# A hybrid decoder step on one core: GpSimd multiplies three key pages of four by the query instead of two

## The chip, the cores and the metric

The kernel runs on one NeuronCore of a Trainium2 chip. The metric is the device time of one launch in microseconds. The engines are TensorE (PE, its weight loads PEld), VectorE (DVE), ScalarE (ACT), GpSimd (POOL) and SyncE (SP, which here issues nearly all DMAs); they run their own instruction streams and meet at semaphores.

## The reference

One layer for 1024 prompt tokens and 8 sample tokens that each have a paged past of 512 keys and values (4 pages of 128). The part that matters here is the samples' attention:

```python
def attend_sample(q, k, v, lam, k_past, v_past):
    s_past = jnp.einsum('bqhcd,bkhcd->bhcqk', q, k_past).astype(F32) * scale
    s_new = jnp.einsum('bqhcd,bkhcd->bhcqk', q, k).astype(F32) * scale
    p = diff_probs(jnp.concatenate([s_past, s_new], axis=-1), lam).astype(v.dtype)
    return (jnp.einsum('bhqk,bkhv->bqhv', p[..., :p_len], v_past)
            + jnp.einsum('bhqk,bkhv->bqhv', p[..., p_len:], v))

# token_mixer: both branches, merged by gates
merged = jax.nn.sigmoid(ga) * ya + jax.nn.sigmoid(gb) * yb
```

There are 8 heads with 2 groups of 64 channels each, so a past key of a sample is a row of 1024 numbers and gives 16 scores.

## The kernel before

The program has four stages, one behind the other: the norm stage, the heads stage (attention and recurrence of the prompt), the **gate stage** (`gates_stage`, L1428) and the tail stage (output projections and the MLP). The gate stage computes the last 12 tiles of the gates ga and gb with TensorE. Tile m is three pieces of 344 columns, so there are 36 pieces; one piece is 8 x 3 matmuls (`product`, L170), since every number is split into a high and a low part (products high x high, high x low, low x high). For each weight tile ScalarE makes the high part (`split`, L1590) and GpSimd the low one (`low`, L1744).

Between the pieces, one of the 8 samples' attention and recurrence steps is worked off every four pieces. `TURN_AT` sets where: at piece 4, 8, 12, ... 28, and 31 for the last. In what follows "turn i" is TensorE's place for sample i. For sample i:

- SyncE loads four key pages (`kp[0]` to `kp[3]`, 128 tokens x 1024), the query row spread over all partitions (`qB`), the sample's recurrent state (`st`), its value row (`vB`) and four value pages (`vp`).
- `keys(i)`: each page is multiplied by `qB` in place, and VectorE sums the product by 64 columns to 16 scores a token (L1783, into `s_tok`). VectorE multiplies pages 0 and 1 (L1779), GpSimd pages 2 and 3 (L1750); VectorE goes through the pages in order and waits for `k_scaled` before it reduces one of GpSimd's.
- TensorE transposes the four score blocks (`turn_scores`, L1673) as soon as the fourth reduction is done (`k_summed`), ahead of piece `TURN_AT[i]`. At sample 5 it also waits for `take_picked(0)`, a copy that VectorE makes right after `keys(5)`.
- VectorE copies the scores (L1823), takes the maximum, ScalarE the exponential (L1620), VectorE normalises, updates the recurrent state with three operations over 128 x 1024 (L1840, L1846, L1848), copies the turned probabilities (L1851), for which TensorE waits with the value products, cuts gate tiles (L1769) and starts `keys(i + 1)`. Behind sample 4 it also selects the values of four samples (L1788, L1790).
- TensorE turns the probabilities one piece after the turn (L1680), and two pieces after it makes the value products (L1691) and the state products (L1699).

All queues are written out by hand. SyncE's order for sample i: key page j of sample i + 1 once reduction j of sample i is done, the query row of i + 1 ahead of page 2, once GpSimd has made its multiplies of sample i (`k_scaled`); weights; then, each behind its wait, the value row, the state (which waits until the state of sample i is stored and used, L1512), and the value pages of i + 1. GpSimd's order: `keys(i + 1)` stands at the piece after turn i, between the low parts of the weights.

Of the kernel before, what the change touches and what calls it, by code (L numbers as in the profile page):

```python
# [44 lines left out]
PAGES = PAST // P  # L45
# [1382 lines left out]
def gates_stage(nc, a, o, c, d, xh, xl, gate, slots, x1):  # L1428
# [3 lines left out]
    with Stage(c) as ctx:  # L1432
# [26 lines left out]
        def S(n, per=1, **k):  # L1459
            return Sig(ctx, nc, f"g_{n}", per=per, **k)  # L1460
# [4 lines left out]
        k_in = [S(f"k_in{i}", step=16) for i in range(PAGES)]  # L1465
        q_in, vb_in, v_in = S("q_in", step=16), S("v_rows_in", step=16), S("v_in", PAGES, step=16)
        st_in, st_out = S("st_in", step=16), S("st_out", step=16)
        k_scaled, k_summed = S("k_scaled", 2), S("k_summed", PAGES)
        new_ready, new_done, new_read = S("new_ready"), S("new_done"), S("new_read")
        s_turned, s_max, s_exp, s_norm = S("s_turned"), S("s_max"), S("s_exp"), S("s_norm")  # L1470
        p_turned, p_read, pv = S("p_turned"), S("p_read"), S("pv")
# [32 lines left out]
        def _(sp):  # L1504
# [3 lines left out]
            def load_keys(i, j):  # L1508
                sp.dma_start(kp[j], flat(a["cache_k"][bass.ds(page_of(i, j), 1)])).then_inc(k_in[j].sem, 16)
# [4 lines left out]
            def load_spread(i):  # L1514

                sp.dma_start(qB, d["q_rows"][bass.ds(i, 1), :].broadcast_to([P, D])).then_inc(q_in.sem, 16)

            def load_values(i):
                sp.dma_start(vB, d["v_rows"][bass.ds(i, 1), :].broadcast_to([P, D])).then_inc(vb_in.sem, 16)
# [5 lines left out]
            def load_weights(m):  # L1525

                if m >= 3:
                    sp.wait_ge(w_hi.sem, w_hi.at(m - 2, 0))
                    sp.wait_ge(w_lo.sem, w_lo.at(m - 2, 0))
                src = wt[bass.ds(m + (3 + NTL * H + GATES_BEFORE), 1)] if m < N_TILES else a["w_mix"][m - N_TILES:m - N_TILES + 1]  # L1530
                sp.dma_start(raw[buf(m)][:, :], flat(src)).then_inc(w_in[buf(m)].sem, 16)

            def load_oa(k):

                sp.dma_start(x1[:, k, 0:T], flat(d["oa"][k:k + 1, :, 0:T])).then_inc(oa_in.sem, 16)
# [10 lines left out]
            for i in range(NS):  # L1546
                for j in range(PAGES):
                    sp.wait_ge(k_summed.sem, k_summed.at(i, j + 1))
                    if i + 1 < NS:
                        if j == 2:  # L1550
                            sp.wait_ge(k_scaled.sem, k_scaled.at(i, 2))
                            load_spread(i + 1)
                        load_keys(i + 1, j)
                if i + 1 == NS:
                    for k in (0, 2, 3, 4, 5):
                        load_oa(k)
                while m < N_TILES + 2 and NP * (m - 3) <= TURN_AT[i] + 1:
                    load_weights(m)
                    m += 1
                sp.wait_ge(st_new.sem, st_new.at(i, 1))  # L1560
                if i + 1 < NS:
                    load_values(i + 1)
                else:
                    load_oa(1)
                if i + 1 < NS:
                    sp.wait_ge(st_out.sem, st_out.at(i, 1))
                    sp.wait_ge(rec_out.sem, rec_out.at(i, 1))
                    load_state(i + 1)
                sp.wait_ge(pv.sem, pv.at(i, 1))
                if i + 1 < NS:  # L1570
                    load_pages(i + 1)
                else:
                    for k in (6, 7):
                        load_oa(k)
# [161 lines left out]
        @block.gpsimd  # L1736
        def _(pool):
            ctx.clear_last(pool)

            def low(m):  # L1740
                weights_in(pool, m)
                weights_free(pool, m)
                pool.wait_ge(w_hi.sem, w_hi.at(m, 0))
                pool.tensor_tensor(wlo[buf(m)][:, :], raw[buf(m)][:, :], whi[buf(m)][:, :].bitcast(F32), ALU.subtract).then_inc(w_lo.sem, 1)  # L1744

            def keys(i):
                pool.wait_ge(q_in.sem, q_in.at(i, 1))
                for j in (2, 3):
                    pool.wait_ge(k_in[j].sem, k_in[j].at(i, 1))
                    pool.tensor_tensor(kp[j], kp[j], qB, ALU.mult).then_inc(k_scaled.sem, 1)  # L1750

            low(1)
            keys(0)
            for n in range(N_PIECES):
                m, j = divmod(n, NP)
                if j == 0 and m:
                    low(m + 1)
                if n - 1 in TURN_AT and TURN_AT.index(n - 1) + 1 < NS:
                    keys(TURN_AT.index(n - 1) + 1)

        @block.vector
        def _(dve):
# [11 lines left out]
            def keys(i):  # L1774
                dve.wait_ge(q_in.sem, q_in.at(i, 1))
                for j in range(PAGES):
                    if j < 2:
                        dve.wait_ge(k_in[j].sem, k_in[j].at(i, 1))
                        ch(dve.tensor_tensor(kp[j], kp[j], qB, ALU.mult))  # L1779
                        ch.sync()  # L1780
                    else:
                        dve.wait_ge(k_scaled.sem, k_scaled.at(i, j - 1))
                    dve.tensor_reduce(s_tok[:, j, :], kp[j].rearrange("p (h n) -> p h n", n=DH), AX.X, ALU.add).then_inc(k_summed.sem, 1)  # L1783

            def select(i):
# [916 lines left out]
```

## Time and profile before

| what | value |
|---|---|
| median of 3 runs | 2424.07 us (2423.71 to 2430.54) |
| the profiled execution: time, span | 2431.48 us, 2429.7 us |
| mean granted clock of TensorE | 0.989 |
| gate stage in the span | 1185 to 1371 us |
| busy: PE, DVE, ACT, POOL | 95%, 66%, 41%, 33% of the span |
| HBM traffic | 83 GB/s over the span; 328 GB/s in the gate stage |

### The profile page before, as it was taken

To read this page: it belongs to the slowest core of one execution; us is meant where nothing else is said; L and a number is where in the kernel's file an instruction comes from. 1 tells how busy PE (TensorE), PEld (TensorE's weight loads), DVE (VectorE), ACT (ScalarE), POOL (GpSimd) and SP (SyncE) were. 2 spreads that over 40 slices of the span, in tenths; PEclk is the share of its full clock that TensorE was granted. 3 is DMA by queue.
4 is the path that set the end of the run, shared out by engine and by line. 5 is a ranking of instruction groups with operands and counts; after the bars stand their busy time and mean duration, and the time that the engine had idled before them with its cause. 6 is when DMAs were issued, how large, how long until landed. Compare 5 with 4: busy or idle time off the path is not lost. (4 is left out here: it accounts for less than half of the span.)

```text
span 2429.7 us, 46021 instructions
## 1 busy us (share of the span) xinstructions
PE 2320.2 (95%) x18425; PEld 2168.3 (89%) x18425; DVE 1611.9 (66%) x2711; ACT 996.2 (41%) x2072; POOL 798.7 (33%) x1019
## 2 busy tenths in 40 slices
PE   7899999899999999899999899999999999999999
PEld 6788888888888888888888799998999999999999
DVE  5568676767767686776778515417876677667667
ACT  6455555656555555655432402114322222222221
POOL 1034251524334251524344214442322232232222
PEclk9999999999999999999999999999999999999999
DMA  6213022221213021221598523111111111111112
GB/s 268 88 37 106 27 72 79 62 80 48 87 52 98 29 91 58 62 89 45 203 340 318 225 87 114 44 56 39 44 44 52 44 44 44 52 44 48 46 47 94
DMA packets 75343, 213.18 MB, mean 88 GB/s; under 512 B 15738, under 2 KB 24186, under 8 KB 75130
## 3 DMA queue, kind: packets, MB, share of 16 engines
q1 hardware_dynamic: 73978, 206.05, 25.1%
q10 hardware_dynamic: 1152, 4.19, 0.4%
q8 instruction: 146, 2.39, 0.4%
q14 instruction: 67, 0.55, 0.1%
HBM read 175.49 MB, written 26.26 MB: 83 GB/s over the span
## 5 line engine op out<-in xcount | busy, mean ns | idle before, releaser
L170 PE MATMUL h_G<-xn_hi,h_w_hi 128*128 128x344 f32 x1392 | 467.8, 336 | 8.4 <-ACT h_d_oraw L858 5.0
L170 PE MATMUL h_G<-xn_hi,h_w_lo 128*128 128x344 f32 x1392 | 445.2, 320 | 0.0
L170 PE MATMUL h_G<-xn_lo,h_w_hi 128*128 128x344 f32 x1392 | 444.9, 320 | 0.0
L2299 POOL TENSOR_TENSOR h_w_lo<-h_w_raw,h_w_hi 128x1024 fp32r<-128x1024 f32 x88 | 212.9, 2420 | 397.4 <-ACT h_w_hi L2070 388.1
L2240 PE MATMUL t_ps<-hn_hi,h_w_hi 128*128 128x344 f32 x1032 | 331.1, 321 | 0.0
L2240 PE MATMUL t_ps<-hn_lo,h_w_hi 128*128 128x344 f32 x1032 | 330.3, 320 | 0.0
L2240 PE MATMUL t_ps<-hn_hi,h_w_lo 128*128 128x344 f32 x1032 | 330.2, 320 | 0.0
L1120 POOL TENSOR_TENSOR h_w_lo<-h_w_raw,h_w_hi 128x1024 fp32r<-128x1024 f32 x58 | 146.3, 2523 | 493.8 <-ACT h_w_hi L738 448.3
L170 PEld LDWEIGHTS h_G<-xn_hi,h_w_hi 128*128 128x128 f32 x1392 | 263.8, 190 | 45.8 <-issue 17.1
L170 PEld LDWEIGHTS h_G<-xn_lo,h_w_hi 128*128 128x128 f32 x1392 | 262.3, 188 | 4.8 <-issue 0.7
L170 PEld LDWEIGHTS h_G<-xn_hi,h_w_lo 128*128 128x128 f32 x1392 | 262.2, 188 | 0.0
L2119 ACT ACTIVATE f_u<-t_ps 128x344 f32<-128x344 f32 x132 | 59.8, 459 | 358.6 <-PE t_ps L2240 358.5
L2384 DVE SCALAR_TENSOR_TENSOR x<-t_ps,keep_mod,x 128x344 f32<-128x344 f32 (+1 forms) x288 | 149.7, 566 | 73.7 <-PE t_ps L170 72.9
L2240 PEld LDWEIGHTS t_ps<-hn_hi,h_w_lo 128*128 128x128 f32 x1032 | 194.5, 188 | 0.0
L2240 PEld LDWEIGHTS t_ps<-hn_lo,h_w_hi 128*128 128x128 f32 x1032 | 194.4, 188 | 0.1
L2240 PEld LDWEIGHTS t_ps<-hn_hi,h_w_hi 128*128 128x128 f32 x1032 | 194.4, 188 | 0.1
L2070 ACT ACTIVATE h_w_hi<-h_w_raw 128x1024 fp32r<-128x1024 f32 x88 | 92.8, 1056 | 233.3 <-PE t_ps L170 224.3
L170 PE MATMUL t_ps<-f_act_hi,h_w_hi 128*128 128x344 f32 x528 | 171.9, 325 | 4.8 <-DVE x L2384 4.7
L170 PE MATMUL t_ps<-f_act_hi,h_w_lo 128*128 128x344 f32 x528 | 169.1, 320 | 0.0
L170 PE MATMUL t_ps<-f_act_lo,h_w_hi 128*128 128x344 f32 x528 | 168.7, 320 | 0.0
L2488 DVE TENSOR_SCALAR f_y<-f_u,keep_vec 128x1024 f32<-128x1024 f32 x44 | 37.8, 860 | 192.8 <-ACT f_u L2119 192.8
L2491 DVE SCALAR_TENSOR_TENSOR f_y<-f_u,keep_vec,f_y 128x1024 f32<-128x1024 f32 x44 | 147.4, 3349 | 1.6
(367 smaller groups left out, 5540.1 us busy)
## 6 DMA issues: line engine op xcount, KB each, us to landing
h_w_raw<-in_w_in SPq DMA_DIRECT2D x72, 512.0 KB, 4.4
h_w_raw<-in_w_ffn SPq DMA_DIRECT2D x66, 512.0 KB, 3.6
h_d_ada_w<-in_w_ada SPq DMA_DIRECT2D x32, 512.0 KB, 5.0
g_kp<-in_cache_k SPq DMA_DIRECT2D x32, 512.0 KB, 7.0
g_vp<-in_cache_v SPq DMA_DIRECT2D x32, 512.0 KB, 5.4
h_w_raw<-in_w_mix SPq DMA_DIRECT2D x24, 512.0 KB, 3.7
x<-in_xT SPq DMA_DIRECT2D x16, 516.0 KB, 7.3
n_ada_w<-in_w_ada SPq DMA_DIRECT2D x16, 512.0 KB, 12.3
```

What stands on the lines that cost most here:

```text
L170: ins = eng.matmul(out, w[:, k * P:(k + 1) * P], x[:, k, columns], start=(k == 0 and n == 0), stop=(k == n_k - 1 and n == 2))
L1120: pool.tensor_tensor(wlo[w][:, :], raw[r][:, :], whi[w][:, :].bitcast(F32), ALU.subtract).then_inc(lo_done.sem, 1)
L2070: act.activation(whi[buf(n)][:, :], raw[n % 2][:, :], ACT.Copy).then_inc(w_hi.sem, 1)
L2119: act.activation(u[s][:, 2 + j * TH:2 + (j + 1) * TH], ffn_bank(t, 0, j), ACT.Copy).then_inc(up_free.sem, 1)
L2240: ins = pe.matmul(ffn_bank(t, 0, j), wp[w][:, k * P:(k + 1) * P], xp[:, k, cols(j)], start=(k == 0 and q == 0), stop=(k == KT - 1 and q == 2))
L2299: pool.tensor_tensor(wlo[buf(n)][:, :], raw[n % 2][:, :], whi[buf(n)][:, :].bitcast(F32), ALU.subtract).then_inc(w_lo.sem, 1)
L2384: ins = dve.scalar_tensor_tensor(out=xt[:, a0:a0 + n], in0=bank[:, 0:n], scalar=gain[:, 0:1], in1=xt[:, a0:a0 + n], op0=ALU.mult, op1=ALU.add)
L2488: ch(dve.tensor_scalar(ys[:, 0:T], us[:, 0:T], w[0], w[3], ALU.mult, ALU.add))
L2491: ch(dve.scalar_tensor_tensor(out=ys[:, 0:T], in0=us[:, 1:1 + T], scalar=w[1], in1=ys[:, 0:T], op0=ALU.mult, op1=ALU.add))
```

## The change

Page 1 of every sample's four key pages is multiplied by the query on GpSimd (ahead of pages 2 and 3) and no longer on VectorE. `k_scaled` counts three a sample, VectorE waits for it before the reductions of pages 1, 2 and 3, and SyncE waits for the third before it loads the next query row.

```diff
-        k_scaled, k_summed = S("k_scaled", 2), S("k_summed", PAGES)
+        k_scaled, k_summed = S("k_scaled", PAGES - 1), S("k_summed", PAGES)
...
                         if j == 2:
-                            sp.wait_ge(k_scaled.sem, k_scaled.at(i, 2))
+                            sp.wait_ge(k_scaled.sem, k_scaled.at(i, PAGES - 1))
                             load_spread(i + 1)
...
             def keys(i):
                 pool.wait_ge(q_in.sem, q_in.at(i, 1))
-                for j in (2, 3):
+                for j in range(1, PAGES):
                     pool.wait_ge(k_in[j].sem, k_in[j].at(i, 1))
                     pool.tensor_tensor(kp[j], kp[j], qB, ALU.mult).then_inc(k_scaled.sem, 1)
...
                 for j in range(PAGES):
-                    if j < 2:
+                    if j < 1:
                         dve.wait_ge(k_in[j].sem, k_in[j].at(i, 1))
                         ch(dve.tensor_tensor(kp[j], kp[j], qB, ALU.mult))
                         ch.sync()
                     else:
-                        dve.wait_ge(k_scaled.sem, k_scaled.at(i, j - 1))
+                        dve.wait_ge(k_scaled.sem, k_scaled.at(i, j))
```

VectorE, `keys` of one sample up to the copy of the scores; the four tiles 17607 to 17610 are the key pages 0 to 3. The piece of difference:

```order
@@ -1477,5 +1476,4 @@
 L1779 TENSOR_TENSOR g_kp_17607<-g_kp_17607,g_qB 128x1024
 L1783 TENSOR_REDUCE g_s_tok<-g_kp_17607 128x16
-L1779 TENSOR_TENSOR g_kp_17608<-g_kp_17608,g_qB 128x1024
 L1783 TENSOR_REDUCE g_s_tok<-g_kp_17608 128x16
 L1783 TENSOR_REDUCE g_s_tok<-g_kp_17609 128x16
```

The multiply of page 1 is gone from between the first and the second reduction; the same in all eight samples.

GpSimd at the start of the gate stage, `keys(0)` and `keys(1)` with the low parts of the weights (`h_w_lo`) around them. Before:

```order
844 L1744 TENSOR_TENSOR h_w_lo_79<-h_w_raw_75,h_w_hi_77 128x1024
845 L1750 TENSOR_TENSOR g_kp_17609<-g_kp_17609,g_qB 128x1024
846 L1750 TENSOR_TENSOR g_kp_17610<-g_kp_17610,g_qB 128x1024
847 L1744 TENSOR_TENSOR h_w_lo_80<-h_w_raw_76,h_w_hi_78 128x1024
848 L1750 TENSOR_TENSOR g_kp_17609<-g_kp_17609,g_qB 128x1024
849 L1750 TENSOR_TENSOR g_kp_17610<-g_kp_17610,g_qB 128x1024
```

And with the change:

```order
844 L1744 TENSOR_TENSOR h_w_lo_79<-h_w_raw_75,h_w_hi_77 128x1024
845 L1750 TENSOR_TENSOR g_kp_17608<-g_kp_17608,g_qB 128x1024
846 L1750 TENSOR_TENSOR g_kp_17609<-g_kp_17609,g_qB 128x1024
847 L1750 TENSOR_TENSOR g_kp_17610<-g_kp_17610,g_qB 128x1024
848 L1744 TENSOR_TENSOR h_w_lo_80<-h_w_raw_76,h_w_hi_78 128x1024
849 L1750 TENSOR_TENSOR g_kp_17608<-g_kp_17608,g_qB 128x1024
```

Page 1 comes first, and what stands behind the keys moves back by one instruction. The orders of the other engines are the same.

## Rows read from the trace of the kernel before

**Rows 1.** Busy time, share of the span and instructions of each engine, page, part 1

```profile
PE 2320.2 (95%) x18425; PEld 2168.3 (89%) x18425; DVE 1611.9 (66%) x2711; ACT 996.2 (41%) x2072; POOL 798.7 (33%) x1019
```

**Rows 2.** Gate stage, busy time by window: length, PE, PEld, DVE, ACT, POOL, clock, DMA, GB/s

```profile
1185.00:1371.00 186.00, 175.40 (x1177) 155.51 (x1177) 144.60 (x196) 65.49 (x94) 74.92 (x28) 0.98 0.88 328
```

**Rows 3.** TensorE's waits in the gate stage: total us, times, longest us

```profile
PE g_Y L1673 <- DVE g_s_tok L1783: 5.7, 4, 2.4
...
PE g_Y L1673 <- DVE keep_s_oa L1795: 3.6, 1, 3.6
```

**Rows 4.** Timeline, TensorE, transposes of samples 0, 2, 3, 5, 7: start, us, [idle before]

```profile
1202.14 0.60 PE L1673 MATMUL g_Y<-keep_ident,g_s_tok 128*16 128x128 f32 x4 [0.88 <-DVE g_s_tok L1783]
...
1241.26 0.60 PE L1673 MATMUL g_Y<-keep_ident,g_s_tok 128*16 128x128 f32 x4 [0.50 <-DVE g_s_tok L1783]
...
1262.53 0.88 PE L1673 MATMUL g_Y<-keep_ident,g_s_tok 128*16 128x128 f32 x4 [1.87 <-DVE g_s_tok L1783]
...
1306.98 0.93 PE L1673 MATMUL g_Y<-keep_ident,g_s_tok 128*16 128x128 f32 x4 [3.63 <-DVE keep_s_oa L1795]
...
1345.81 0.60 PE L1673 MATMUL g_Y<-keep_ident,g_s_tok 128*16 128x128 f32 x4 [2.43 <-DVE g_s_tok L1783]
```

**Rows 5.** Timeline, VectorE, copy of the scores in samples 1, 2 and 4

```profile
1222.00 0.68 DVE L1823 COPY g_sc<-g_Y 16x512 f32<-16x512 f32 x1 [3.37 <-PE g_Y L1673]
...
1241.90 0.68 DVE L1823 COPY g_sc<-g_Y 16x512 f32<-16x512 f32 x1 [0.70 <-PE g_Y L1673]
...
1283.96 0.68 DVE L1823 COPY g_sc<-g_Y 16x512 f32<-16x512 f32 x1 [3.05 <-PE g_Y L1673]
```

**Rows 6.** SyncE's longest wait in the gate stage

```profile
SPq L1512 <- DMA out_s_state<-g_st: 30.9, 7, 6.4
```

**Rows 7.** Instructions on the key pages: duration ns min/median/max, first and last start

```profile
L1783 DVE TENSOR_REDUCE g_s_tok<-g_kp x32: 1206/1220/1221, 1194.9 to 1344.5; 128x16 f32<-128x1024 f32 x32
...
L1779 DVE TENSOR_TENSOR g_kp<-g_kp,g_qB x16: 1218/1694/3414, 1193.6 to 1339.6; 128x1024 f32<-128x1024 f32 x16
...
L1750 POOL TENSOR_TENSOR g_kp<-g_kp,g_qB x16: 2372/2778/3415, 1195.1 to 1341.1; 128x1024 f32<-128x1024 f32 x16
```

**Rows 8.** Timeline, VectorE and GpSimd, keys of sample 3

```profile
1254.00 1.23 DVE L1779 TENSOR_TENSOR g_kp<-g_kp,g_qB 128x1024 f32<-128x1024 f32 x1 [3.58 <-DMA g_qB<-q_rows]
...
1255.49 5.73 POOL L1750 TENSOR_TENSOR g_kp<-g_kp,g_qB 128x1024 f32<-128x1024 f32 x2 [10.71 <-DMA g_kp<-in_cache_k]
...
1256.40 2.57 DVE L1779 TENSOR_TENSOR g_kp<-g_kp,g_qB 128x1024 f32<-128x1024 f32 x1
...
1259.00 3.47 DVE L1783 TENSOR_REDUCE g_s_tok<-g_kp 128x16 f32<-128x1024 f32 x3
```

**Rows 9.** Timeline, VectorE and GpSimd, end of sample 4 and keys of sample 5

```profile
1293.46 1.23 DVE L1848 TENSOR_TENSOR g_st<-g_st,g_vB 128x1024 f32<-128x1024 f32 x1
...
1294.57 5.18 POOL L1750 TENSOR_TENSOR g_kp<-g_kp,g_qB 128x1024 f32<-128x1024 f32 x2 [2.22 <-DMA g_kp<-in_cache_k]
...
1294.60 2.90 DVE L1769 TENSOR_SCALAR gate_b<-gate_b 128x1032 f32<-128x1032 f32 x1
...
1297.42 3.41 DVE L1779 TENSOR_TENSOR g_kp<-g_kp,g_qB 128x1024 f32<-128x1024 f32 x1
...
1303.26 3.47 DVE L1783 TENSOR_REDUCE g_s_tok<-g_kp 128x16 f32<-128x1024 f32 x3
```

**Rows 10.** Windows of one microsecond, TensorE: length, busy, granted clock, DMA, GB/s

```profile
1263.00:1264.00 1.00, 1.00 (x5) 0.50 0.76 295
...
1346.00:1347.00 1.00, 1.00 (x9) 1.00 0.90 356
```

**Rows 11.** VectorE's wait for the query row, whole gate stage

```profile
DVE g_kp L1779 <- DMA g_qB<-q_rows: 7.0, 5, 3.6
```

**Rows 12.** Timeline, VectorE and TensorE, probabilities and value products of sample 0

```profile
1209.75 0.28 DVE L1851 COPY g_pt<-g_Y 128x128 f32<-128x128 f32 x1
...
1211.42 1.92 PE L1691 MATMUL g_V<-g_vp,g_pt 128*32 128x512 f32 x16
```

## The prediction

> **What bounds the kernel now.** I read the busy shares first: TensorE is busy for 2320.2 of 2429.7 us [rows 1], so what the change does counts only where it makes TensorE wait or spares it a wait. The stretch of the gate stage comes next: from 1185 to 1371 us TensorE works 175.4 of 186 us, VectorE 144.6 and GpSimd 74.9 [rows 2]. Both changed engines have spare time there in sum; the order inside a sample decides.
>
> Then the waits of TensorE in that stretch: 5.7 us in four waits for the last reduction of a sample's keys (L1783), and 3.6 us for `take_picked`, which VectorE runs right behind the keys of sample 5 [rows 3]. Together 9.3 us, at the score transposes (L1673). In order of time they are 0.88 us at sample 0, 0.50 at 2, 1.87 at 3, 3.63 at 5 and 2.43 at 7 [rows 4]. At samples 1, 4 and 6 it is the other way round: VectorE idles before its copy of the scores for 3.37 and 3.05 us at 1 and 4 (6 is like them), where 0.70 is what the copy takes to follow a late transpose. So the keys were ready 2.7 and 2.35 us early [rows 5].
>
> So in five samples of eight **the end of the key chain sets when TensorE goes on**, and all that the stage can gain from faster keys is 9.3 us plus what the clock costs behind such waits.
>
> Last, why the keys are late at all. SyncE waits 30.9 us in seven waits until the state of the sample before has been stored [rows 6], and the next value pages, key pages and query row are queued behind that wait. The load for sample i+2 thus hangs on the turn of sample i: the transposes of 2 and 0 lie 39.1 us apart, of 3 and 1 some 41.2 (that of 1 is 0.64 us before its copy, as 1241.26 is before 1241.90), of 7 and 5 38.8 [rows 4, 5]. A delay at one turn reaches the turn after the next, and the delays of one parity add up.
>
> **The change, part by part.** VectorE loses eight multiplies, one a sample, with their chain steps; GpSimd gains eight, ahead of the two it has. No transfer is added. SyncE waits for a third multiply before it overwrites the query row. The page that moves is page 1, so VectorE's second reduction now waits for GpSimd, and so do its third and fourth.
>
> *What one multiply costs on either engine.* A multiply takes VectorE 1.22 us at its fastest, and 3.41 at its slowest; GpSimd takes 2.37 at its fastest, 3.41 at its slowest, 2.78 in the middle. The reductions are always 1.21 to 1.22 [rows 7]. The spread has a pattern, seen in sample 3: GpSimd's two multiplies take 5.73 us together, and VectorE's multiply of page 1 starts inside the first (1256.40), takes 2.57 and ends at 1258.97 [rows 8]. That is VectorE waiting for the first GpSimd multiply to end and GpSimd's second waiting for VectorE: 2 x 2.37 + 0.99 = 5.73. The two never multiply at once, and the reductions disturb nobody. The Trainium skill (SBUF — State Buffer, section "SBUF: two separate sides") says that the pair of ports these engines share is locked for a whole instruction and the loser blocks; by that rule the trace agrees. Were the interference a slowdown that stayed when VectorE's multiply goes, three multiplies of 2.78 and more would take 8.3 to 8.7 us.
>
> *The key chain after.* Before, in sample 3, from VectorE's first multiply (1254.00, at which the query row has just landed) to the end of the last reduction (1259.00 + 3.47 = 1262.47) are 8.47 us: GpSimd starts 1.49 in, works 5.73, and the last reduction adds 1.25. After, GpSimd works 3 x 2.37 = 7.11, with no VectorE multiply in between: 1.49 + 7.11 + 1.25 = 9.85, which is 1.38 later. If GpSimd wins the ports first, at the landing, VectorE's first multiply falls between its first and second: 2.37 + 1.1 + 4.74 + 1.25 = 9.46, 1.0 later. **I take 1.3 us a sample**, between 1.0 and 1.4; with the slowed multiply of 2.78 it would be up to 2.9. On VectorE the chain is no shorter for it: its own work falls from 4 reductions and 2 multiplies to 4 and 1, but it waits for GpSimd before each of the last three. The multiply taken from VectorE thus buys nothing at the end.
>
> *Sum over the samples.* Turn 0: +1.2 (GpSimd starts with page 1 behind VectorE's first multiply, about where it started before). Turn 1: TensorE arrives 1.2 later by itself, and the keys have 2.7 to spare: +1.2. Turn 2 follows the loads that hang on turn 0: 1.2 + 1.3 = +2.5. Turn 3 hangs on turn 1: +2.5. Turn 4 has slack 2.35: it moves with TensorE, +2.5. Turn 5: +2.5 and a term of its own, below. Turn 6 has slack: no more. Turn 7 hangs on turn 5 and adds 1.3.
>
> *Turn 5.* There VectorE is late (it also selects the values of four samples), and GpSimd multiplies before it does: GpSimd starts at 1294.57, VectorE's addition ends at 1294.69, its cut of a gate tile takes 2.90, its first multiply 3.41, and the last reduction ends at 1306.73 [rows 9]. After, GpSimd can start when the query row and page 1 are in, an estimated 1.5 us earlier (what lies in sample 3 between landing and start). Either the addition goes first: GpSimd, cut, GpSimd, multiply (to 1301.0), GpSimd to 1303.4, two reductions behind: 1305.9, which is 0.8 earlier than the 1306.73 of now. Or GpSimd goes first and the addition, cut and multiply are pushed between and behind its three: the multiply ends at 1303.2 and four reductions follow to 1308.1, 1.4 later. I take +0.3.
>
> *Clock.* Behind the waits of 1.87 and 3.63 us the granted clock is at its lower level, 1.2 GHz, 0.50 from 1263 us on [rows 10], and the transposes take 0.88 and 0.93 instead of 0.60; behind 2.43 us it stayed at 2.4 GHz (1.00 from 1346 on), behind 0.88 and 0.50 too [rows 4, 10]. The price: from turn 3 to 4 and 5 to 6, with the fall, 20.8 us; from 0 to 1, without, 19.2; so 1.5 us. The wait at 7 grows to 3.7, longer than both that were followed by a fall: I count one more fall, +1.5, and none elsewhere.
>
> *Costed at nothing.* The weight splits of GpSimd (L1744) stand behind the keys and start up to 1.3 us later; TensorE shows no wait for them in the stage [rows 3], and by the program each stands three pieces ahead of its product; without that cover they cost their delay. The later release of the query row only counts in sample 0 (SyncE reaches that wait late elsewhere, behind the stores), where it is inside the +1.3 that turn 2 inherits. The stage ends with TensorE, so its delay passes on whole to the last stage.
>
> Sum: 2.5 + 0.3 + 1.3 + 1.5 = **5.6 us**. The profiled execution took 2431.5 us and would take 2437.1; the median of the runs shown is 2424.1, and by it the forecast is 2429.7 us, 0.23% more. What a measurement of this kernel can tell from no change is about 0.3%, 7.3 us.
>
> **Rivals.**
> *Slower by more: GpSimd gets in front of VectorE's writes.* VectorE waited for the query row in five samples only [rows 11]; in 1 and 5 it lands while VectorE still updates the state. If GpSimd takes the ports at that moment, the addition (L1848) is 2.4 us late, and the copy of the probabilities behind it on VectorE, for which TensorE waits with the values. That copy ends at 1210.03 in sample 0 and the value products start at 1211.42 [rows 12], so 1.4 us are spare; with 2.4 late, turn 1 moves 1.0 more, turn 3 with it, and turn 5 takes its +1.4, 1.1 more than counted. If the wait at 0, grown to 2.1 us, is also followed by a fall of the clock (1.87 was), 1.5 more goes through turns 1 and 3. 5.6 + 1.0 + 1.1 + 1.5 = 9.2 us: 2433.3. For it: the 3.41 and 2.90 in sample 5 show exactly such pushing. Against it: the moments of landing must fit, and 2.43 us passed without a fall. It decides from 1.7 us above my sum.
>
> *No loss: turn 5 and the clock pay it back.* The addition goes first at 5 (-1.1 against my sum), no fall at 7 (-1.5), and one of the falls at 3 or 5 doesn't come (-1.5): 1.5 us, 2425.6. Inside 0.3%.
>
> *Faster: the multiply off VectorE is what shortens the chain.* The Trainium skill (GPSIMD Engine Reference, its opening) calls GpSimd the wrong choice for elementwise arithmetic, VectorE about twice as fast, which speaks against this way. By the rows it would need page 1 so early that GpSimd is through with it before the query row's landing, which cannot be where VectorE waits for that row itself. Only samples 1 and 5 leave room, and a gain over 7.3 us needs nearly all of the 9.3 us of waits gone: 2424.1 - 8 = 2416.
>
> *The change doesn't act:* excluded by the order of instructions, which shows the eight multiplies moved.
>
> **How the numbers follow.** My forecast, 3 to 7 us more: 0.48. The rival with the loss paid back, from -2 to +3: 0.16. GpSimd in front, over 7.3 us: 0.31. Faster: 0.05. From the sum's forecast the scatter of the shown runs (2423.7 to 2430.5) can shift either way. Slower by over 0.3%: 0.31; within 0.3%: 0.64; faster: 0.05. The range reaches down to the rival with the loss paid back (+1.5) less 3 for the scatter, and up to the slower one (+9.2) with 3 more: 2422.5 to 2436, rounded.
>
> **What would show it.** The waits of TensorE at L1673 grow: about 2.1, 1.8, 1.9, 3.9 and 3.7 us at samples 0, 2, 3, 5 and 7. GpSimd's multiplies at L1750 number 24 and the middle one is 2.4 us, no longer 2.78. From VectorE's first multiply to the end of the last reduction are 9.5 to 9.9 us in samples 2, 3, 4, 6 and 7. VectorE shows waits for GpSimd before its second, third and fourth reductions. The stage, from 1185 to 1371, becomes some 5 us longer, and nothing else does. I am wrong if the waits at L1673 don't grow (the chain was then not bound by GpSimd), or if a wait appears at L1744, the values or the state products that is not there now.

## The result and the profile after

| kernel | median of 12 runs | lowest to highest |
|---|---|---|
| before | 2425.65 us | 2423.71 to 2430.54 |
| changed | 2430.62 us | 2427.05 to 2439.88 |

The ratio is 1.0019, with an interval of 1.0011 to 1.0026: the change costs 4.6 us by the ratio and 5.0 by the medians. The runs tell that from nothing, and it lies within the 0.3% that the prediction counts as no difference. The profiled execution of the changed kernel took 2439.88 us, the slowest of its runs; TensorE's first piece of the gate stage starts 5.1 us later in it than in the profile before, ahead of anything the change touches. Only the stage itself is compared below, and with more profiles than one.

The page, part 1, of the changed kernel, the gate stage in one window of the same length, and TensorE's waits in it (as [rows 1], [rows 2] and [rows 3]):

```profile
PE 2327.5 (95%) x18425; PEld 2175.9 (89%) x18425; DVE 1607.4 (66%) x2703; ACT 995.5 (41%) x2072; POOL 819.0 (34%) x1027
```

```profile
1190.00:1376.00 186.00, 174.63 (x1158) 154.84 (x1159) 139.10 (x185) 62.54 (x91) 96.22 (x36) 0.96 0.87 328
```

```profile
PE g_Y L1673 <- DVE g_s_tok L1783: 8.0, 4, 3.7
...
PE g_SO L1699 <- DVE g_st L1848: 2.2, 1, 2.2
...
PE g_Y L1673 <- DVE keep_s_oa L1795: 0.8, 1, 0.8
```

GpSimd's busy time in the stage goes from 74.9 to 96.2 us, VectorE's from 144.6 to 139.1. The mean clock of the stage falls from 0.98 to 0.96. The waits for the keys go from 5.7 to 8.0 us; the one for `take_picked` (sample 5) has nearly gone, and a new one of 2.2 us is there, for the state of sample 4. At the score transposes (L1673) they are 8.8 us together, where it was 9.3: by this one profile they didn't grow. Over more profiles they did: 9.3 and 6.9 us in the two of before, 8.8, 10.4 and 11.1 in the three of the change.

The transposes of samples 0, 2, 3, 5 and 7 on the timeline, as [rows 4]:

```profile
1208.22 0.60 PE L1673 MATMUL g_Y<-keep_ident,g_s_tok 128*16 128x128 f32 x4 [1.85 <-DVE g_s_tok L1783]
...
1247.18 0.60 PE L1673 MATMUL g_Y<-keep_ident,g_s_tok 128*16 128x128 f32 x4 [0.34 <-DVE g_s_tok L1783]
...
1268.67 0.60 PE L1673 MATMUL g_Y<-keep_ident,g_s_tok 128*16 128x128 f32 x4 [2.08 <-DVE g_s_tok L1783]
...
1313.80 0.60 PE L1673 MATMUL g_Y<-keep_ident,g_s_tok 128*16 128x128 f32 x4 [0.81 <-DVE keep_s_oa L1795]
...
1352.42 1.02 PE L1673 MATMUL g_Y<-keep_ident,g_s_tok 128*16 128x128 f32 x4 [3.70 <-DVE g_s_tok L1783]
```

The waits are 1.85, 0.34, 2.08, 0.81 and 3.70 us, where they were 0.88, 0.50, 1.87, 3.63 and 2.43. And the instructions on the key pages, as [rows 7]:

```profile
L1783 DVE TENSOR_REDUCE g_s_tok<-g_kp x32: 1208/1220/1221, 1200.0 to 1351.1; 128x16 f32<-128x1024 f32 x32
...
L1750 POOL TENSOR_TENSOR g_kp<-g_kp,g_qB x24: 2334/2631/3441, 1198.9 to 1348.8; 128x1024 f32<-128x1024 f32 x24
...
L1779 DVE TENSOR_TENSOR g_kp<-g_kp,g_qB x8: 1223/2312/3422, 1198.7 to 1343.0; 128x1024 f32<-128x1024 f32 x8
...
  POOL g_kp L1750: 14.3, 13
```

The last line is what VectorE's reductions waited for GpSimd, total and times. GpSimd's middle multiply is 2.63 us and the shortest 2.33: the middle one still holds waiting for the ports. Sample 3, VectorE and GpSimd, as [rows 8]:

```profile
1259.18 1.23 DVE L1779 TENSOR_TENSOR g_kp<-g_kp,g_qB 128x1024 f32<-128x1024 f32 x1 [2.68 <-DMA g_qB<-q_rows]
...
1259.22 8.13 POOL L1750 TENSOR_TENSOR g_kp<-g_kp,g_qB 128x1024 f32<-128x1024 f32 x3 [8.37 <-DMA g_qB<-q_rows]
...
1260.44 1.22 DVE L1783 TENSOR_REDUCE g_s_tok<-g_kp 128x16 f32<-128x1024 f32 x1
...
1262.70 1.22 DVE L1783 TENSOR_REDUCE g_s_tok<-g_kp 128x16 f32<-128x1024 f32 x1 [1.04 <-POOL g_kp L1750]
...
1265.06 1.22 DVE L1783 TENSOR_REDUCE g_s_tok<-g_kp 128x16 f32<-128x1024 f32 x1 [1.14 <-POOL g_kp L1750]
...
1267.39 1.22 DVE L1783 TENSOR_REDUCE g_s_tok<-g_kp 128x16 f32<-128x1024 f32 x1 [1.11 <-POOL g_kp L1750]
```

Both engines start at the query row's landing. VectorE gets the ports first (its multiply takes an undisturbed 1.23 us), GpSimd's three take 8.13, its first blocked for about 1 us. Each of VectorE's last three reductions waits 1.0 to 1.15 us for GpSimd. From VectorE's multiply to the end of the last reduction are 1267.39 + 1.22 - 1259.18 = 9.43 us, where it was 8.47. GpSimd is the chain from end to end.

**Where the turns stand.** With the two profiles of before and three of the change that I have by the end (e10, e11 and e12 below are the repeats), the start of each turn's transposes, in us from the first piece's first matmul, averaged; the last column is the start of the last piece's last matmul. The two lower rows set single profiles of gated kernels beside one another (e5 and e7, e6 and e9 below), which differ only by who multiplies page 1:

| | turn 0 | 1 | 2 | 3 | 4 | 5 | 6 | 7 | last matmul |
|---|---|---|---|---|---|---|---|---|---|
| before (2) | 17.0 | 36.2 | 55.8 | 76.8 | 96.9 | 118.9 | 140.5 | 158.8 | 182.8 |
| changed (3) | 18.1 | 37.9 | 57.7 | 78.2 | 98.3 | 121.0 | 141.4 | 160.6 | 186.8 |
| difference | 1.1 | 1.7 | 1.9 | 1.4 | 1.4 | 2.1 | 0.9 | 1.8 | 4.0 |
| e7 less e5 | 1.3 | 1.2 | 1.9 | 0.6 | 1.0 | 2.4 | 1.6 | 3.3 | 4.9 |
| e9 less e6 | 1.0 | 1.0 | 0.9 | 0.5 | 0.5 | 1.8 | 1.8 | 3.0 | 2.2 |

The averages differ by 4.0 us at the end, 1.8 of them up to turn 7 and 2.2 behind it, though behind it TensorE has the same five pieces and waits for nothing more. That is near the loss of the medians, but the average is a weak one: turn 7 stands at 160.6 and 157.1 us in the two profiles of before and at 162.1, 158.9 and 160.9 in the three of the change. The 1.8 isn't told from this scatter, and the two gated pairs have 3.3 and 3.0 there. At turns 3 and 4 no comparison has more than 1.4.

**What stands behind turn 7** is the clock. From turn 7 to the last matmul are 24.04 and 23.96 us in the profiles before; 26.46, 25.51 and 26.59 in those of the change. One-microsecond windows of TensorE, changed kernel (length, busy, granted clock, DMA share, GB/s):

```profile
1350.00:1351.00 1.00, 0.00 (x0) 1.00 0.56 82
...
1352.00:1353.00 1.00, 0.58 (x3) 0.50 0.76 291
...
1355.00:1356.00 1.00, 1.00 (x5) 0.50 0.94 336
...
1358.00:1359.00 1.00, 1.00 (x9) 1.00 1.06 434
```

TensorE was idle 3.70 us before turn 7. The granted clock fell in that wait, just after 1351, and TensorE ran at 1.2 GHz (0.50) until 1358. In the profile before, the wait there was 2.43 us and the clock stayed at 2.4 GHz [rows 10].

### The profile page after: what moved, and what is told of

It reads as the page before. It is cut to its first block and busy times, and to the rows that moved or that the text cites. A ratio compares the mean times of both kernels' runs of the same rounds, so it can differ in the third digit from the quotient of the medians.

```text
span 2438.1 us, 46021 instructions
## 1 busy us (share of the span) xinstructions
PE 2327.5 (95%) x18425; PEld 2175.9 (89%) x18425; DVE 1607.4 (66%) x2703; ACT 995.5 (41%) x2072; POOL 819.0 (34%) x1027
```

## The experiments

Each was timed against the kernel before on its own chip, in five rounds where nothing else is said. Each has twelve runs, e2 seven, e6 nine, e11 and e12 one. The order of SyncE, the semaphores and the number of multiplies are what they vary.

### e1: only the lighter half

```diff
-                        ch(dve.tensor_tensor(kp[j], kp[j], qB, ALU.mult))
-                        ch.sync()
+                        if j == 0:
+                            ch(dve.tensor_tensor(kp[j], kp[j], qB, ALU.mult))
+                            ch.sync()
```

> The multiply of page 1 is taken from VectorE and given to nobody (page 1's scores are then the plain sums of its keys); GpSimd keeps pages 2 and 3. This is the half of the change that lightens VectorE, by itself. Theory (GpSimd's multiplies end the key chain, VectorE's multiply only delays them through the shared ports): GpSimd's two multiplies take 4.8 us a sample in place of 5.73, and from VectorE's first multiply to the last reduction there are 7.5 us in place of 8.47. Each late turn gains up to 1 us: TensorE's waits at L1673 fall from 9.3 us to about 5, the time by 2 to 5 us (2421 to 2424 where before is 2425.7). Rival (VectorE's own work is the chain): the chain loses VectorE's whole 2.57 us, the waits nearly vanish, 6 us or more are gained.

Measured: 2424.81 us, 0.9991 of before (0.9980 to 1.0002). The gain of 1.8 us isn't told from none, and is just below the 2 to 5 expected; the time alone decides nothing. The mechanism shows in the profile, sample 2:

```profile
1233.67 1.22 DVE L1780 TENSOR_TENSOR g_kp<-g_kp,g_qB 128x1024 f32<-128x1024 f32 x1 [1.44 <-DMA g_qB<-q_rows]
...
1235.00 4.76 POOL L1750 TENSOR_TENSOR g_kp<-g_kp,g_qB 128x1024 f32<-128x1024 f32 x2 [3.33 <-DMA g_kp<-in_cache_k]
```

GpSimd's two multiplies take 4.76 us in place of 5.73, and the last reduction ends at 1241.02, 7.35 us behind VectorE's multiply. So taking VectorE's multiply away shortens the chain by about 1 us, which is the time it held the ports, not by the 2.43 us that its row in sample 2 of before shows. The rival, that VectorE is the chain, falls: it asked for 6 us.

### e2: only the heavier half

```diff
                     pool.wait_ge(k_in[j].sem, k_in[j].at(i, 1))
+                    if j == 2 and i != 5:
+                        pool.tensor_tensor(sel[:, :, :].rearrange("p h v -> p (h v)"), kp[j], qB, ALU.mult)
```

> The other half by itself, pushed further: before GpSimd multiplies page 2 it multiplies it once more into a tile that is free then (all samples but sample 5), VectorE keeps its two multiplies. Theory: GpSimd starts where it does before (page 2 lands 1.49 us behind the query row), then has 3 x 2.37 plus 0.99 for VectorE's multiply: 10.8 us to the last reduction in place of 8.47. The late turns come up to 2.4 us later, waits behind which the clock falls get more: slower by 7 to 14 us, against 5 for the change. Rival (GpSimd has room, the query row's landing alone decides): within 2 us of before.

Measured: 2437.26 us, 1.0046 (1.0029 to 1.0062), 11 us slower, within the 7 to 14 expected. Sample 4, where both waited for their loads (L1781 is VectorE's multiply, L1751 GpSimd's added one, L1785 the reductions):

```profile
1275.08 1.23 DVE L1781 TENSOR_TENSOR g_kp<-g_kp,g_qB 128x1024 f32<-128x1024 f32 x1 [0.31 <-DMA g_qB<-q_rows]
...
1276.53 2.40 POOL L1751 TENSOR_TENSOR g_sel<-g_kp,g_qB 128x1024 f32<-128x1024 f32 x1 [9.23 <-DMA g_kp<-in_cache_k]
...
1282.30 1.22 DVE L1785 TENSOR_REDUCE g_s_tok<-g_kp 128x16 f32<-128x1024 f32 x1 [1.03 <-POOL g_kp L1752]
```

From VectorE's first multiply to the end of the last reduction (1285.87) are 10.79 us, as worked out. TensorE's waits at 0 and 7 become 3.17 and 4.98 us. GpSimd has no room in this chain; a multiply more on it is a later turn.

### e3 and e4: the keys earlier

SyncE loads the next value pages before it waits for the state's store; e3 with two multiplies on GpSimd, e4 with the change's three.

```diff
+                sp.wait_ge(pv.sem, pv.at(i, 1))
+                if i + 1 < NS:
+                    load_pages(i + 1)
                 if i + 1 < NS:
                     sp.wait_ge(st_out.sem, st_out.at(i, 1))
                     sp.wait_ge(rec_out.sem, rec_out.at(i, 1))
                     load_state(i + 1)
-                sp.wait_ge(pv.sem, pv.at(i, 1))
-                if i + 1 < NS:
-                    load_pages(i + 1)
                 else:
```

> Only SyncE's order is changed, on the kernel before: the value pages of the next sample are loaded once they are free, ahead of the wait for the state's store and the load of the next state. The next key pages and query row then stand behind one 0.5 us issue after that wait, no longer behind the four value pages (5.5 us). Theory (the late turns come from the late query row, which hangs on that wait): the query row lands some 4 us earlier, TensorE's waits at L1673 fall from 9.3 us to under 2 and the clock falls behind them go: 8 to 13 us faster (2413 to 2418). Rival (transfers share the bandwidth, the keys are late whatever the order): within 3 us of before.

> The same order of SyncE on the changed kernel. Theory: with the keys early by more than the 1 us that the third multiply costs, the change costs nothing: within 1.5 us of the run with the same order and two multiplies on GpSimd (e3). Rival (GpSimd pushing VectorE's state updates is what costs): GpSimd now starts more often while VectorE updates the state, TensorE waits for the state or the probabilities, and it is 3 us or more slower than e3.

Measured: e3 2434.78 us, 1.0032 (1.0021 to 1.0043), slower by 8 us where 8 to 13 faster was expected; e4 2431.42 us, 1.0026 (1.0014 to 1.0038), 3.4 us under e3 by the medians, with intervals that overlap. e3's expectation was wrong, rival and theory both; e4 isn't slower than e3, so its rival falls, but it doesn't show what it was built to show, since the keys weren't early in either. e3's profile says why. Sample 4, VectorE and then GpSimd:

```profile
1270.23 2.87 DVE L1769 TENSOR_SCALAR gate_a<-gate_a 128x1032 f32<-128x1032 f32 x1
...
1273.02 3.40 DVE L1779 TENSOR_TENSOR g_kp<-g_kp,g_qB 128x1024 f32<-128x1024 f32 x1
...
1277.59 2.17 DVE L1779 TENSOR_TENSOR g_kp<-g_kp,g_qB 128x1024 f32<-128x1024 f32 x1
...
1279.79 3.47 DVE L1783 TENSOR_REDUCE g_s_tok<-g_kp 128x16 f32<-128x1024 f32 x3
...
1270.15 5.18 POOL L1750 TENSOR_TENSOR g_kp<-g_kp,g_qB 128x1024 f32<-128x1024 f32 x2 [8.70 <-DMA g_kp<-in_cache_k]
```

The loads did come early: nothing here waits for one except GpSimd's start. GpSimd now starts first, at 1270.15, while VectorE has the gate cut before it. The cut takes 2.87 us (0.69 alone), the first multiply 3.40 (1.22 alone), the second 2.17, this one behind a weight split of GpSimd. GpSimd is through at 1275.33, and the keys are ready only at 1283.26: here **VectorE is the end of the chain**, because it was made to wait for the ports three times. The same sample in e4:

```profile
1268.17 2.68 DVE L1769 TENSOR_SCALAR gate_a<-gate_a 128x1032 f32<-128x1032 f32 x1
...
1270.78 3.42 DVE L1779 TENSOR_TENSOR g_kp<-g_kp,g_qB 128x1024 f32<-128x1024 f32 x1
...
1274.23 4.60 DVE L1783 TENSOR_REDUCE g_s_tok<-g_kp 128x16 f32<-128x1024 f32 x4
...
1267.40 9.06 POOL L1750 TENSOR_TENSOR g_kp<-g_kp,g_qB 128x1024 f32<-128x1024 f32 x3 [6.89 <-DMA g_qB<-q_rows]
```

From VectorE's first multiply to the end of the last reduction are 1274.23 + 4.60 - 1270.78 = 8.05 us against 10.24 in e3. Where GpSimd goes first, VectorE's multiply of page 1 is worth having off VectorE. The two are opposite cases: the change lengthens this chain by 1 us where both wait for the query row and shortens it by up to 2 where GpSimd is ahead. The Trainium skill (SBUF — State Buffer, section "SBUF: two separate sides") counts among the VectorE instructions that contend those with two inputs in SBUF and those in a two-port mode; the rows agree as to which are held up: the multiplies and the cut are, the reductions never (1.21 to 1.23 us in every profile).

### e5 and e6: VectorE first

GpSimd waits for VectorE's first multiply of the sample (a semaphore `k_first`); e5 is the kernel before with it, e6 has SyncE's order of e3 too.

```diff
             def keys(i):
                 pool.wait_ge(q_in.sem, q_in.at(i, 1))
+                pool.wait_ge(k_first.sem, k_first.at(i, 1))
...
-                        ch(dve.tensor_tensor(kp[j], kp[j], qB, ALU.mult))
-                        ch.sync()
+                        ins = dve.tensor_tensor(kp[j], kp[j], qB, ALU.mult)
+                        if j == 0:
+                            ins.then_inc(k_first.sem, 1)
+                            dve.wait_ge(k_first.sem, k_first.at(i, 1))
+                        else:
+                            ch(ins)
+                            ch.sync()
```

> The kernel before, and GpSimd starts a sample's multiplies only once VectorE's first one is done (a semaphore more). Theory (GpSimd ahead of VectorE pushes VectorE's state update, gate cut and first multiply by up to 2.2 us each): in samples 2, 3, 4, 6 and 7 page 2 lands later than that anyway, nothing changes; in sample 5 VectorE's cut and multiply take 0.7 and 1.2 us in place of 2.9 and 3.4, the keys are ready 3 us earlier, the wait of 3.6 us and the clock fall behind it go: 2 to 5 us faster than before. Rival (nothing but the query row's landing counts): within 1 us of before.

> The same with SyncE's order of e3 (value pages ahead of the wait for the state's store), two multiplies on GpSimd. Theory: e3 got its keys early and lost it because GpSimd then went first. With VectorE first a sample's keys end 8.5 us after VectorE is free, 18.3 us behind the turn before, and TensorE comes back after 19.2: the waits at samples 2, 3, 4 and 6 go, what stays is about 1 us at 0, 1 to 2 at 5 and 3 at 7. 5 to 9 us faster than before, 12 or more faster than e3. Rival (the early loads themselves disturb, by bandwidth or by SyncE's queue): as slow as e3, 8 us over before.

Measured: e5 2424.10 us, 0.9992 (0.9981 to 1.0003): 2.5 us less by the medians, and not told from nothing. In its profile sample 5's wait is 0.47 us; but so it is in the second profile of the kernel before (e11: 0.45). There VectorE's first multiply started at 1293.65 and took 1.22, and GpSimd, which waited for key page 2, came behind it:

```profile
1294.99 5.75 POOL L1750 TENSOR_TENSOR g_kp<-g_kp,g_qB 128x1024 f32<-128x1024 f32 x2 [4.20 <-DMA g_kp<-in_cache_k]
```

So whether GpSimd pushes VectorE in sample 5 depends on when page 2 lands and how far VectorE is, and the gate removes a loss that not every execution has.

e6: **2421.14 us, 0.9972 (0.9959 to 0.9985)**, 5.5 us faster than before by the medians and 13.6 faster than e3 (on another chip), the best of all kernels here. Its sample 3, the same instructions as in e3's rows above:

```profile
1253.95 0.69 DVE L1771 TENSOR_SCALAR gate_b<-gate_b 128x1032 f32<-128x1032 f32 x1
...
1254.56 1.22 DVE L1781 TENSOR_TENSOR g_kp<-g_kp,g_qB 128x1024 f32<-128x1024 f32 x1
...
1256.94 2.43 DVE L1781 TENSOR_TENSOR g_kp<-g_kp,g_qB 128x1024 f32<-128x1024 f32 x1
...
1259.40 3.49 DVE L1790 TENSOR_REDUCE g_s_tok<-g_kp 128x16 f32<-128x1024 f32 x3
...
1255.91 5.74 POOL L1752 TENSOR_TENSOR g_kp<-g_kp,g_qB 128x1024 f32<-128x1024 f32 x2 [6.90 <-DVE g_kp L1781]
```

The cut takes 0.69 and the first multiply 1.22; the keys are ready 8.33 us behind it, and VectorE then idles 2.24 us before its copy. TensorE's waits for the keys:

```profile
PE g_Y L1674 <- DVE g_s_tok L1790: 2.4, 2, 1.3
...
PE g_Y L1674 <- DVE keep_s_oa L1802: 0.5, 1, 0.5
...
PE g_V L1692 <- DVE g_pt L1858: 1.8, 2, 1.0
```

2.4 us at samples 0 and 7, 0.5 at 5; new are 1.8 us for the copy of the probabilities. The rival, that early loads disturb by themselves, falls: e6 has them as e3 has.

### e7: the change, VectorE first

The change with the gate of e5.

> The changed kernel with the same gate: GpSimd's three multiplies start behind VectorE's one. The chain is 1.25 + 3 x 2.37 + 1.25 = 9.6 us in every sample, 0.2 longer than in the change where both wait for the query row, and nothing of VectorE's is pushed in samples 1, 2, 5 and 6. If the change's 5 us come mostly from the longer chain, this is as slow as the change, +4 to +6 us over before; if they come from the pushing (the state update of sample 4, 3.27 us for 1.23, with TensorE's wait of 2.2 us), it is +1 to +3.

Measured: 2431.42 us, 1.0015 (1.0006 to 1.0024), as slow as the change. Sample 6, both behind the query row:

```profile
1317.95 1.23 DVE L1781 TENSOR_TENSOR g_kp<-g_kp,g_qB 128x1024 f32<-128x1024 f32 x1 [2.60 <-DMA g_qB<-q_rows]
...
1319.31 7.10 POOL L1752 TENSOR_TENSOR g_kp<-g_kp,g_qB 128x1024 f32<-128x1024 f32 x3 [10.88 <-DVE g_kp L1781]
```

GpSimd's three take 7.10 us, undisturbed, and the chain to the last reduction (1327.66) is 9.71. No state update is pushed, the 2.2 us of TensorE's wait for the state are gone, and the loss stays: **it is the longer chain that costs**, and the pushing isn't needed for it. This chain is itself 0.3 us longer than the change's 9.43, so what the pushing costs besides isn't told.

The cleanest measure of the multiply is e7 beside e5: one chip, GpSimd behind VectorE in both, and only page 1 changes hands. The medians are 2431.42 and 2424.10 us, 7.3 apart, 0.23% by the ratios, and the intervals don't meet. The chain in sample 4 goes from 8.36 to 9.71 us. TensorE's waits for the keys (L1790) in e5 and then in e7, total, times, longest:

```profile
PE g_Y L1674 <- DVE g_s_tok L1790: 5.7, 4, 2.8
...
PE g_Y L1674 <- DVE g_s_tok L1790: 9.4, 6, 3.5
```

With the wait for `take_picked` they are 6.2 and 11.2 us.

### e8: the opposite change

```diff
-                for j in (2, 3):
+                for j in (3,):
...
-                    if j < 2:
+                    if j < 3:
```

(with `k_scaled` counting one a sample).

> The opposite change: GpSimd multiplies page 3 alone, VectorE pages 0, 1 and 2. VectorE's own work becomes the chain, 3 x 1.22 + 4 x 1.22 = 8.6 us and about 1 to 2 us where one of its multiplies waits for GpSimd's: 9 to 10.5 us from the query row, in place of 8.47, so as long as with three pages on GpSimd. Theory (both sides are balanced at two pages): +3 to +7 us over before. Rival (any multiply on GpSimd costs more than on VectorE, by speed): faster than before.

Measured: 2429.98 us, 1.0011 (1.0000 to 1.0022), 3.4 us over before, with an interval that reaches down to none. In samples 3 and 4 the chain from the first multiply is 9.32 and 9.34 us (10.37 and 10.12 in samples 1 and 2); in sample 3 the third of VectorE's multiplies takes 2.17, behind GpSimd's. Two pages a side has the shortest chain of the three where VectorE waited for the query row: 9.3, 8.45 and 9.4 us for one, two and three pages on GpSimd.

### e9: the change with early keys and VectorE first

The change, the gate of e5 and SyncE's order of e3: e6 with the third multiply.

> The changed kernel with both: GpSimd behind VectorE's first multiply, and SyncE's value pages ahead. Beside e6 it differs only by who multiplies page 1. Theory (the chain from VectorE's first multiply, 9.7 against 8.5 us, counts where TensorE has no slack): VectorE is free for the keys 9 to 9.5 us behind a turn, so they are ready 18.8 to 19.2 behind it, just before TensorE at samples 1 to 4 and 6, and 1.2 us later than in e6 at 0, 5 and 7, where it waits: 2 to 5 us slower than e6. Rival (the multiply costs its full 1.2 us in every sample): 9 us or more slower than e6. Other rival (with early keys it is free): within 1 us.

Measured: 2427.15 us, 0.9997 (0.9985 to 1.0009), level with before; e6 is at 0.9972. The difference is 0.25%, 6 us, across two chips, and with both intervals some 2 to 10 us; the 2 to 5 expected lie in that. TensorE waits 2.11 us at 0, 0.79 at 2, 1.80 at 5 and 2.53 at 7, where e6 waits 1.10, 0, 0.47 and 1.27; samples 1, 3, 4 and 6 have no wait in either. So the multiply is free where there is slack and costs 0.8 to 1.3 us at four turns, 4.4 in all. Turn 7 stands 3.0 us later. The stages of the two profiles, 179.1 and 176.9 us, differ by 2.2 only, since behind turn 7 e6 waits 0.8 us more, for the probabilities; the rest of the 6 isn't accounted for.

### e10, e11 and e12: how far one profile carries

The changed kernel again (e10, five rounds), and before and changed once more untimed but for one run each (e11, e12).

> The change itself once more, on the chip of e9 and with another profile. The time is 4 to 6 us over before. Where the clock falls is expected to vary from one execution to another: the profile taken first shows it behind turns 3 and 7 and behind the state products of sample 4, and below full speed for 6.9 us behind turn 7 where before it was 3.4 to 4.6 us at a time. If this profile's stage is as long as that one's (188.5 us from the first to the last piece) with fewer falls, the waits alone make it; if it is 2 us or more shorter, the falls are part of the loss and of the scatter.

> The kernel before once more, for a second profile on one chip with e12. The key chain from VectorE's first multiply (where it waited for the query row) to the last reduction is again 8.4 to 8.5 us, page 2 is again what GpSimd waits for. If single profiles of one kernel can be set beside one another, the stage from its first to its last piece is again 184.6 us within 1; if the falls of the clock and the landings shift it, by 2 us and more.

> The change, third profile, on the chip of e11. The chain is 9.3 to 9.5 us where both engines waited for the query row. The stages of the two profiles so far are 188.5 and 184.4 us. With 2 us or more over e11's, the stage alone shows the loss that the medians show; with less, single profiles can't carry it and only the medians do.

Measured: e10 2429.63 us, 1.0014 (1.0002 to 1.0026), 3.4 us over before, the change once more. The stage from first to last matmul is 184.6 and 181.1 us in the two profiles of before, 188.5, 184.4 and 187.5 in those of the change: one execution differs from the next by 4 us, as much as the change does. The profiles of e10 and of the kernel before, set beside one another, would have shown no loss. The falls of the clock are a part of the scatter: three in the stage of the first profile of the change, one in e10's, which is 4.1 us shorter, and two in e12's; two in the first profile of before, one in e11's. e11 was to have 184.6 within 1 if single profiles can be compared, and has 181.1; e12 over e11 shows 6.4 us, more than the runs have. What does repeat is the chain where VectorE waited for the query row. Sample 4 of e11, VectorE's first multiply and its last three reductions; then sample 4 of e12, VectorE's multiply and GpSimd's three:

```profile
1273.31 1.23 DVE L1779 TENSOR_TENSOR g_kp<-g_kp,g_qB 128x1024 f32<-128x1024 f32 x1 [2.31 <-DMA g_qB<-q_rows]
...
1278.24 3.48 DVE L1783 TENSOR_REDUCE g_s_tok<-g_kp 128x16 f32<-128x1024 f32 x3
```

```profile
1277.52 1.23 DVE L1779 TENSOR_TENSOR g_kp<-g_kp,g_qB 128x1024 f32<-128x1024 f32 x1 [2.03 <-DMA g_qB<-q_rows]
...
1277.57 8.14 POOL L1750 TENSOR_TENSOR g_kp<-g_kp,g_qB 128x1024 f32<-128x1024 f32 x3 [9.95 <-DMA g_qB<-q_rows]
```

8.41 us in sample 4 before (1281.72 - 1273.31), 9.44 changed (the last reduction ends at 1286.96). Five samples gave 8.36 to 8.52 in the first profile before, 8.32 to 8.90 in e11; those of the change that waited for the row, in its three profiles, 9.38 to 9.46.

The clock behind turn 7, over all profiles (wait of TensorE at the turn, then turn 7 to the last matmul):

| | wait at turn 7, us | to the last matmul, us | clock fell |
|---|---|---|---|
| e5 | 0.27 | 23.95 | no |
| e11 (before) | 1.41 | 23.96 | no |
| before | 2.43 | 24.04 | no |
| e9 | 2.53 | 23.96 | no |
| e4 | 2.92 | 25.5 | yes |
| e10 (change) | 3.25 | 25.51 | yes |
| e7, e8 | 3.54, 3.53 | 25.5 | yes |
| change, e12 | 3.70, 3.79 | 26.46, 26.59 | yes |
| e2, e3 | 4.98, 5.23 | 26.6, 25.3 | yes |

Left out are e1 and e6, which have another wait behind turn 7.

## Why the prediction was right, and which of its steps were off

**The forecast** was 5.6 us, 0.23%, within 0.3%; measured are 4.6 us, 0.19%. The mechanism is shown: GpSimd ends the key chain (e1, e2), the change makes it longer by one GpSimd multiply less what VectorE's held the ports for (8.36 to 9.71 us, e5 and e7), and TensorE has no slack at several turns. How that becomes a time was forecast less well than the total says.

**The signs it gave.** Not all came. GpSimd's multiplies number 24, but the middle one is 2.63 us and not 2.4. The chains of samples 2, 3, 4, 6 and 7 are 9.27, 9.43, 9.44, 8.04 and 9.38 us, all under the 9.5 to 9.9 named. Two signs of being wrong can be read in the first profile: the waits at L1673 fell from 9.3 to 8.8 us, and a wait of 2.2 us for the state products is new. Neither holds over the profiles: the waits at L1673 average 8.1 us before and 10.1 with the change (6.2 and 11.2 in e5 and e7), and the state products wait 0.2 us in e10 and e12, as before.

**The key chain, +1.3 us a sample: 0.96 measured.** I took GpSimd's start 1.49 us behind the landing as fixed. It was page 2's arrival; page 1 is in before the query row, and GpSimd now starts at 0.04. (Sample 0 is different: GpSimd waits for page 1 there, and the chain is 9.43, 9.42 and 10.26 us in the three profiles of the change.) Neither of my two orders came: VectorE's multiply wins the ports, GpSimd follows it directly, 9.43 us in all, next to the lower end (9.46). The bound at that end, 1.0, was the right value, and its reason (who comes first) only half right.

**The slowed multiply of 2.78 us, up to +2.9: no.** The multiplies take 2.3 to 2.4 us where nothing is between them (7.10 for three in e7). The row's middle value held waiting as well as work.

**The sum over the turns: +4.1 at turn 7; 1.8 in the averages, 3.3 and 3.0 in the gated pairs.** Here the working failed in part. I let a delay at turn 0 reach turn 2 and one at turn 1 reach turn 3, with 1.3 added each time. Turn 0 moved by 1.0 to 1.3, as predicted with 1.2. But turns 3 and 4 stand only 0.5 to 1.4 later in the three comparisons, where 2.5 was forecast. The query row of sample 3 doesn't follow turn 1: in the eight profiles in which VectorE waited for it, it landed 67.1 to 68.8 us behind the stage's first matmul, while turn 1 stood anywhere from 35.3 to 37.4, and both 35.3 (e1) and 37.0 (e8) had it at 67.1. Toward the end it does follow: the row of sample 7 moved from 146.1 to 153.1 us as turn 5 moved from 114.0 to 123.7 (e1 and e2, the ends of ten profiles), and between turns 5 and 7 neither pair lost what it had: e7 and e9 add 0.9 and 1.2 us there. So the delay adds up late in the stage and not early. What sets the landing of the early rows wasn't tested.

**The clock, +1.5 behind turn 7: 2.2 measured, and the best step of the prediction.** The wait at 7 was to grow to 3.7 us, longer than all that a fall had followed; it is 3.70, 3.25 and 3.79, and the clock fell in all three and in neither profile before. The term was too small because the low clock lasts 6.8 to 6.9 us in two of the three, while the falls in the profile before, from which I priced it, lasted 3.4; in e10 it is 3.4 too, and costs 1.5. I also left the other falls as they were: ahead of turn 7 there are 2 and 1 in the profiles before and 2, 0 and 1 in those of the change, so part of the price comes back there. And the rule behind the step, that a longer wait is followed by a fall, doesn't hold everywhere: e2 waited 3.61 us at turn 5 and its clock stayed at 2.4 GHz:

```profile
1310.00:1311.00 1.00, 1.00 (x9) 1.00 0.90 352
```

By the averages the two errors, 2.3 too much and 0.7 too little, went against each other; the total is better than its terms, and that is luck.

**Turn 5, +0.3.** In the first profile of the change GpSimd went in front of the state's addition, as the slower rival said:

```profile
1299.55 3.27 DVE L1848 TENSOR_TENSOR g_st<-g_st,g_vB 128x1024 f32<-128x1024 f32 x1
```

That is 3.27 us for 1.23, with TensorE waiting 2.2 for the state, and this wait took the place of most of the turn's own (0.81). In e10 and e12 it didn't happen. The turn stands 2.1 later on average, with a spread of 5.6 us between the profiles of before and 4.7 between those of the change.

**The rivals.** The slower one (GpSimd in front of VectorE's writes, 9.2 us) shows in sample 4's state in one profile of three, but e7, which rules it out, is no faster; the loss doesn't need it. (e3 and e4 show the same wait for the state, 2.3 and 2.2 us.) The faster one is refused where both engines wait for the query row, yet it has a case: in e3 and e4, with GpSimd ahead, the same change shortens the chain and the medians go down by 3.4 us, though not clear of their intervals.

**A wait at the weight splits** didn't appear, as costed. **The reductions** wait for GpSimd as predicted where VectorE goes first, 13 times, 14.3 us in all.

## What to carry to other kernels

Where two engines hold each other up as VectorE's and GpSimd's multiplies do here, an instruction's longest or middle duration in the rows holds waiting too: the price of moving one is its shortest duration on the new engine less the time that the old one held the ports, and who starts first decides which engine ends the chain. Before balancing such a pair, look who goes first and try to fix the order with a semaphore: with early loads that was worth 13.6 us by the medians (e6 beside e3), alone nothing that the runs tell (e5). Of a delay that is handed from turn to turn through loads, look in several profiles whether the landing moves with the turn before adding it up: here it did at sample 7 and not at sample 3. Of a longer wait on TensorE ask if the clock may fall behind it, since in the averaged stages the fall was 2.2 of the 4.0 us. And where one execution differs from the next by as much as the change does, one profile of each can't show the loss.

## What was not expected of the hardware

- An early load can cost: e3's earlier keys made the kernel 8 us slower, since GpSimd, released earlier, took the ports in front of VectorE's cut (2.87 us for 0.69) and multiply (3.40 for 1.22). The weight splits of GpSimd block in the same way (2.17 for 1.22).
- At turn 7 the granted clock was at 1.2 GHz for 6.8 to 6.9 us in two of the three profiles of the change and in e2, of which TensorE worked 5.5 us and more, and for 3.4 us in e10. The length doesn't follow the wait: behind e3's 5.23 us, the longest, it was 3.4.
- At the same turn no wait up to 2.53 us was followed by a fall and each from 2.92 us on was; elsewhere it isn't so clean: a wait of 2.08 us at turn 3 of the change (first profile) was followed by one, and 2.11 at turn 0 of e9, 2.77 at turn 6 of e1 and 3.61 at turn 5 of e2 weren't.
